# A two-layer hybrid decoder trunk on one core: one layer end for all layers, and two GpSimd subtractions moved to VectorE

## The reference, cut to what matters

```python
for l in range(2):
    sh_m, sc_m, g_m, sh_f, sc_f, g_f = split(silu(c) @ ada_w[l] + ada_b[l], 6)
    proj = (rms_norm(x, norm_mix_g[l]) * (1 + sc_m) + sh_m) @ w_in[l]
    y = concatenate([ssd(proj), mla(proj), moba(proj)])      # 512 + 256 + 256 columns, normalised by group
    x = x + g_m * (y @ w_out[l])                             # the output projection
    hf = rms_norm(x, norm_ffn_g[l]) * (1 + sc_f) + sh_f
    x = x + g_f * moe_ffn(hf, ...)                           # 16 experts, each token goes to two of them
```

## Time and profile before

| What | Value |
|---|---|
| Time, median of 3 runs (lowest, highest) | 1483.41 us (1477.52, 1484.29) |
| The profiled execution's own time | 1484.28 us |
| Its span, first to last instruction | 1482.5 us |
| PE busy | 1331.1 us (90%) |
| PEld busy | 1050.8 us (71%) |
| DVE busy | 1165.1 us (79%) |
| ACT busy | 735.0 us (50%) |
| POOL busy | 257.7 us (17%) |
| Mean granted TensorE clock | 0.949 of full speed |

### The profile page before, as it was taken

How to read it: one execution, slowest core, us unless ns; L and a number is a source line. 1 busy time by engine, 2 the same in 40 slices (tenths; PEclk the granted TensorE clock), 3 DMA queues, 4 the chain that set the end, 5 groups by cost and what they waited for, 6 DMA issues and landing times. The chain is left out here.

```text
span 1482.5 us, 17406 instructions
## 1 busy us (share of the span) xinstructions
PE 1331.1 (90%) x6467; PEld 1050.8 (71%) x6467; DVE 1165.1 (79%) x1372; ACT 735.0 (50%) x967; POOL 257.7 (17%) x300
## 2 busy tenths in 40 slices
PE   6799987869989999999949998886898999999994
PEld 3677865657878888888647777564677788888882
DVE  3669856894679999999855987398657899999985
ACT  1334343562337777777413342345413777777760
POOL 0100135461011000000120012339001110010002
PEclk9899997989999999999969999898899999999997
DMA  9676521423579999998548573133327899999955
GB/s 361 234 263 225 191 92 56 142 88 141 211 285 365 413 401 416 410 407 351 210 164 301 172 256 118 57 114 114 128 99 284 336 399 410 404 415 403 410 186 185
DMA packets 95461, 378.64 MB, mean 255 GB/s; under 512 B 5961, under 2 KB 8759, under 8 KB 85768
## 3 DMA queue, kind: packets, MB, share of 16 engines
q1 hardware_dynamic: 71816, 307.83, 54.7%
q0 software_dynamic: 15232, 55.63, 9.6%
q10 hardware_dynamic: 8320, 13.96, 2.7%
HBM read 344.58 MB, written 32.82 MB: 255 GB/s over the span
## 5 line engine op out<-in xcount | busy, mean ns | idle before, releaser
L1278 PE MATMUL ps<-mod_rounded,work_rounded 128*128 128x512 f32 x340 | 136.9, 403 | 1.1 <-DVE work_rounded L2284 1.1
L1280 PE MATMUL ps<-mod_rounded,work_rounded 128*128 128x512 f32 x340 | 134.6, 396 | 0.0
L1739 DVE SCALAR_TENSOR_TENSOR gain<-ring,csil,gain 128x512 f32<-128x512 f32 x134 | 111.6, 833 | 3.3
L1279 PE MATMUL ps<-ring_rounded,work_rounded 128*128 128x512 f32 x288 | 113.9, 396 | 0.0
L2143 DVE TENSOR_TENSOR ring_rounded<-ring,mod_rounded 128x2048 fp32r<-128x2048 f32 (+1 forms) x54 | 102.9, 1930 | 1.4
L1279 PE MATMUL ps<-work_rounded 128*128 128x512 f32 x256 | 101.0, 395 | 0.0
L2143 DVE TENSOR_TENSOR work_rounded<-work,mod_rounded 128x2048 fp32r<-128x2048 f32 (+1 forms) x48 | 91.3, 1931 | 9.9 <-ACT mod_rounded L1638 8.7
L2527 POOL DMA_INDIRECT work<-ffn_rows,slot_idx x34 | 42.0, 1236 | 302.8 <-PE ps L1264 270.1
L929 PE MATMUL ps<-ring_rounded,actT_rounded 128*128 128x512 f32 (+1 forms) x256 | 93.9, 367 | 0.0
L1638 ACT ACTIVATE mod_rounded<-ring 128x2048 fp32r<-128x2048 f32 (+1 forms) x54 | 85.9, 1625 | 0.0
L929 PE MATMUL ps<-work_rounded,mod_rounded 128*128 128x512 f32 (+1 forms) x192 | 77.1, 401 | 4.0 <-ACT work L1405 4.0
(11 more groups left out here) (371 smaller groups left out, 3647.2 us busy)
## 6 DMA issues: line engine op xcount, KB each, us to landing
ring<-in_ada_w SPq DMA_DIRECT2D x38, 1024.0 KB, 5.3
ring<-in_moe_w_gate SPq DMA_DIRECT2D x18, 2048.0 KB, 10.0
ring<-in_moe_w_up SPq DMA_DIRECT2D x18, 2048.0 KB, 10.4
ring<-in_moe_w_down SPq DMA_DIRECT2D x18, 2048.0 KB
work<-in_moe_w_up SPq DMA_DIRECT2D x16, 2048.0 KB, 10.7
work<-in_moe_w_down SPq DMA_DIRECT2D x16, 2048.0 KB, 11.6
work<-in_moe_w_gate SPq DMA_DIRECT2D x16, 2048.0 KB, 10.2
expert_rows<-work POOLq DMA_DIRECT2D x32, 512.0 KB, 7.9
```

What stands on the lines that cost most here:

```text
L1278: pe.matmul(ps[j][:, :], xl, hi, start=k == 0, stop=False)
L1279: pe.matmul(ps[j][:, :], xh, lo, start=False, stop=False)
L1280: mm = pe.matmul(ps[j][:, :], xh, hi, start=False, stop=k == KD - 1)
L1739: add(v.scalar_tensor_tensor(acc, w, csil[:, k:k + 1], acc, ALU.mult, ALU.add))
```

## The change

1. The low halves (0, 1) and (1, 0) of the output weights are made by VectorE: (0, 1) in step n = 25 of the heads, (1, 0) after the last early `y_low` and ahead of the wait for the norm. GpSimd's loop and its semaphore are gone, and PE waits for `out_w_lo` to reach 1, 2, 3, 4 in the order of the halves.
2. At the layer's end the branches on L are gone from SP, ScalarE and VectorE: layer 1 too loads "the next layer's" first block (of layer 0 again), rows and gain, splits the block and scales the gain. Nothing reads these.
3. The eight adds of slot 16 and their products stand once, after `If(nov > 1)` instead of before it. Within that branch each further tile first adds the tile before it.

```diff
-                with sp.If(L < DEPTH - 1):
-                    load_first_in(sp, (L + 1) % DEPTH)
-                    sp.dma_start(mod[:, 0:2 * D], ...).then_inc(next_b, 16)
-                    sp.wait_ge(y_ps, 2 * (NTL - 1))
-                    load_mix_gain(sp, (L + 1) % DEPTH)
-                    sp.wait_ge(next_b, 16)
+                load_first_in(sp, (L + 1) % DEPTH)
+                sp.dma_start(mod[:, 0:2 * D], ...).then_inc(next_b, 16)
+                sp.wait_ge(y_ps, 2 * (NTL - 1))
+                load_mix_gain(sp, (L + 1) % DEPTH)
+                sp.wait_ge(next_b, 16)
...
-                OUT_LOW = [(out_w_lo, 1), (out_w_lo_g, 1), (out_w_lo_g, 2), (out_w_lo, 2)]
-                            pe.wait_ge(*OUT_LOW[2 * b + k // 4])
+                            pe.wait_ge(out_w_lo, 2 * b + k // 4 + 1)
...
-                for b in range(2):
-                    pe.wait_ge(y_ev, 2 * (NTL - 1) + b + 1)
-                    for t in range(T):
-                        by_token(b, t).then_inc(cb_ps, 1)
                 with pe.If(nov > 1):
...
+                for b in range(2):
+                    pe.wait_ge(y_ev, 2 * (NTL - 1) + b + 1)
+                    for t in range(T):
+                        by_token(b, t).then_inc(cb_ps, 1)
...
-                with a.If(L < DEPTH - 1):
-                    a.wait_ge(y_ps, 2 * (NTL - 1))
-                    first_in_hi(a)
+                a.wait_ge(y_ps, 2 * (NTL - 1))
+                first_in_hi(a)
...
-                    if n == 19:
-                        out_weights_lo(0, 0)
+                    if n in (19, 25):
+                        out_weights_lo(0, (n - 19) // 6)
                     late_adds(n)
...
                     y_low(q)
+                out_weights_lo(1, 0)
                 v.wait_ge(yrs, 3)
...
-                with v.If(L < DEPTH - 1):
-                    last_out(True)
-                with v.If(L > DEPTH - 2):
-                    last_out(False)
+                e = NTL - 1
+                first_in_lo(v, 0, 2 * (len(IN_ORDER) - 1))
+                y_out(e, e % 2, halves=(0,))
+                first_in_lo(v, 1, 2 * (len(IN_ORDER) - 1))
+                y_out(e, e % 2, halves=(1,))
+                v.wait_ge(next_b, 16)
+                mix_gain(v)
                 with v.If(nov > 1):
...
+                for b in range(2):
+                    for t in range(T):
+                        v.wait_ge(cb_ps, T * b + t + 1)
+                        add_by_token(0, b, t)
...
-                for b, half in ((0, 1), (1, 0)):
-                    g.wait_ge(out_w_hi, 2 * b + half + 1)
-                    raw, lo, hi = out_part(b, half)
-                    g.tensor_tensor(lo, raw, hi.bitcast(F32), ALU.subtract).then_inc(out_w_lo_g, 1)
```

More of the change, by code:

```diff
@@ L832, in _ @@
                 sp.wait_ge(row_st[2], 16)
-                with sp.If(L < DEPTH - 1):
-                    load_first_in(sp, (L + 1) % DEPTH)
-                    sp.dma_start(mod[:, 0:2 * D], mod_rows[bass.ds(L + 1, 1), 0:2 * D].broadcast_to([P, 2 * D])
-                                 ).then_inc(next_b, 16)
-                    sp.wait_ge(y_ps, 2 * (NTL - 1))
-                    load_mix_gain(sp, (L + 1) % DEPTH)
-                    sp.wait_ge(next_b, 16)
+                load_first_in(sp, (L + 1) % DEPTH)
+                sp.dma_start(mod[:, 0:2 * D], mod_rows[bass.ds(L + 1, 1), 0:2 * D].broadcast_to([P, 2 * D])
+                             ).then_inc(next_b, 16)
+                sp.wait_ge(y_ps, 2 * (NTL - 1))
+                load_mix_gain(sp, (L + 1) % DEPTH)
+                sp.wait_ge(next_b, 16)
                 nov = sp.value_load(ctl[0:1, 0:1], min_val=0, max_val=NOV)
@@ L1330, in by_token @@
                                      start=True, stop=True)
-                for b in range(2):
-                    pe.wait_ge(y_ev, 2 * (NTL - 1) + b + 1)
-                    for t in range(T):
-                        by_token(b, t).then_inc(cb_ps, 1)
                 with pe.If(nov > 1):
+                    pe.wait_ge(y_ev, 2 * NTL)
                     with pe.Fori(0, NOV - 1) as i:
                         with pe.If(nov > i + 1):
+                            for b in range(2):
+                                for t in range(T):
+                                    by_token(b, t).then_inc(cb_ps, 1)
                             pe.wait_ge(ov_x, i + 1)
@@ L2327, in add_by_token @@
                     return v.scalar_tensor_tensor(x_, ps[2 * t + b][:, :], over_w[:, t, n:n + 1], x_, ALU.mult, ALU.add)
[L2329 to L2344, removed]
                 hidden(NTL - 1)
@@ L2359, in _ @@
                         with v.If(nov > n):
+                            for b in range(2):
+                                for t in range(T):
+                                    v.wait_ge(cb_ps, 2 * T * (n - 1) + T * b + t + 1)
+                                    ins = add_by_token(n - 1, b, t)
+                            ins.then_inc(ov_x, 1)
                             v.wait_ge(ov_si, n)
@@ L2363, in _ @@
                             slot_tokens(n)
+                            v.wait_ge(ov_x, n)
+                            v.tensor_copy(over_w[:, :, 0:1], over_w[:, :, n:n + 1])
                             v.wait_ge(ov_yp, n)
@@ L2366, in _ @@
                             v.tensor_tensor(ysb[:, 0, 512:1024], ps[7][:, :], gf[:, 512:1024], ALU.mult).then_inc(ov_ye, 1)
-                            for b in range(2):
-                                for t in range(T):
-                                    v.wait_ge(cb_ps, 2 * T * n + T * b + t + 1)
-                                    ins = add_by_token(n, b, t)
-                            ins.then_inc(ov_x, 1)
+                            v.wait_ge(cb_ps, 2 * T * (n + 1))
+                for b in range(2):
+                    for t in range(T):
+                        v.wait_ge(cb_ps, T * b + t + 1)
+                        add_by_token(0, b, t)
             @block.gpsimd
```

1 line of the change is left out of this document (removed).

## The result

| | Before | After |
|---|---|---|
| Time, median of 5 runs (lowest, highest) | 1483.41 us (1477.52, 1485.46) | 1472.33 us (1469.03, 1477.23) |
| The profiled execution's own time | 1484.28 us | 1472.33 us |
| Its span | 1482.5 us | 1470.7 us |
| DVE busy | 1165.1 us | 1162.9 us |
| POOL busy | 257.7 us | 239.1 us |

The ratio is 0.9934, with a 95% interval from 0.9912 to 0.9957: faster by 11 us, beyond the 0.5% that the forecast wanted. The forecast was 1472.7.

A forecast was written before the change was run, and what follows sets the result against it. In the heads VectorE, held up by GpSimd's subtractions, was taken to bound all engines. -15.6 + 4.6 + 0 - 1.0 + 0 + 1.3 = -10.7 us from 1484.28 gives 1473.6, as a median 1472.7; range 1465.5 to 1479.5.

The forecast's parts named there:

- GpSimd's subtractions gone, half (0, 1) in step 25: Heads, both layers: -15.6 us of VectorE waiting under GpSimd, +4.6 us for VectorE making the half itself.
- the prediction's sign: Heads: biased(28) 5.3 us earlier after the heads' start in layer 0, 5.7 in layer 1; output products 5 to 6 earlier.
- Half (1, 0) at no cost: After the last early column block: VectorE's 2.29 us fit its 2.95 us wait for GpSimd's norm, cost 0.
- The slow clock behind the hole: Heads, after PE's idle stretch: part of the low granted clock goes, -0.5 us per layer, -1.0 in sum.
- End of layer 0: Layer 0's end: GpSimd arrives last and covers what moves on VectorE and PE, 0 us, bounds -3.0 and +3.0.
- rival 2: Layer ends: the skips were dear, -3 us in layer 0 and -1 in layer 1, 1467.4 us; chance 0.12.
- End of layer 1: Layer 1's end: loads delay gathers by 4.4 us, barrier 1.8 us later less a 0.5 us skip, +1.3 us.
- rival 1: Layer ends: uncovered skip before PE's products, +1 us in layer 0, +4.4 in layer 1, total 1477; chance 0.17.
- the prediction's own signs: Layer 1's end: right if 5 to 7 us follow the last add; wrong if down-products-to-next-layer time changes over 3 us.
- The hole: Heads: stretch where GpSimd's subtractions hold up VectorE and PE idles 8.10 us in layer 0, 7.49 in layer 1.
- rival 3: Heads: the hole is not the path, so the 11 us are only moved, 1483 us; chance 0.06.
- Rival 4: Layer 1's end: slot 16's products wait for the useless 2 MB load, 11.2 us later, 1483.9 us; chance 0.04.

The follow-up runs named there:

- e1: The kernel before with only the move of the two low halves to VectorE, layer ends as before: 1472.72 us, ratio 0.9946 to the kernel before.
- e2: The kernel before with only the new layer end; GpSimd keeps its two subtractions: 1484.35 us, ratio 1.0020 to the kernel before.
- e7: The changed kernel with half (0, 1) back on GpSimd, half (1, 0) still on VectorE: 1476.46 us, ratio 0.9968 to the kernel before.
- e6: The changed kernel with half (1, 0) back on GpSimd, half (0, 1) still on VectorE: 1490.12 us, ratio 1.0039 to the kernel before.
- e0: The repetition: the changed kernel run once more, unaltered, beside the other variants: 1476.42 us, ratio 0.9959 to the kernel before.
- e5: The kernel before with the move alone, half (0, 1) in step 24, layer ends as before: 1469.08 us, ratio 0.9898 to the kernel before.
- e8: The changed kernel with two extra VectorE instructions of 1.22 us before slot 16's adds: 1478.22 us, ratio 0.9962 to the kernel before.
- e3: The changed kernel with the branches on L back, slot 16's adds still behind If(nov > 1): 1472.83 us, ratio 0.9945 to the kernel before.
- e10: The changed kernel with layer 1's 2 MB block load and split branched out again, rows and gain still loaded: 1472.91 us, ratio 0.9937.

## Why the prediction was right

**What the forecast was against what came.** 1472.7 was predicted; the first pair gave 1472.33, and the ratio of the repetition, 0.9959, puts it near 1477. Both lie in the range. "Faster" (below 1476.0) holds by the first pair; by the repetition the change gives 0.4% and falls just short of it. The mechanism of the gain was right, two terms were mis-sized (the end of layer 1 for a wrong reason), and luck hid it: of the 11.8 us between the two traces only 7.6 net lie in stretches that the change touches.

- **GpSimd's subtractions gone, half (0, 1) in step 25 (-15.6 + 4.6).** Right. `biased(28)` was to come 5.3 and 5.7 us earlier; it came 4.9 and 5.8, counted from step 24. Counted from the start of the heads, as the prediction's sign has it, it came 3.6 and 10.4 us earlier, because steps 0 to 4 ran at other clocks. The output products start 4.7 and 6.3 us earlier after step 24 (at 333.11 and 1039.68 for 336.80 and 1056.25), for the 5 to 6 of the sign. The half took 2.29 us as the earlier trace rows had it, the sums shrank to the medians of the earlier trace rows. `e1` and `e2` separate it from the rest, `e7` and `e6` repeat the blocking with one subtraction each.
- **Half (1, 0) at no cost.** Right. It lies in the wait for the norm, which comes 336.47 - 333.06 = 3.4 us after the column block instead of 2.95: GpSimd's first small norm instruction took 0.66 us instead of 0.20 (the kernel before, at 338.35) and ended just behind VectorE's half. That cost nothing: from step 31 to the last down products both traces take 399.0 us in layer 0 and 399.2 in layer 1. The Trainium skill ("SBUF — State Buffer", section "SBUF: two separate sides") says that a VectorE instruction with two SBUF inputs and a GpSimd one that reads SBUF exclude one another for a whole instruction; that fits these rows and those of `e6`. The blocked instruction of `e7`, a TENSOR_SCALAR, has one such input, as has the first long one of the earlier trace rows, so where the prediction lets the rows of the long sums agree with that rule, this holds for the other three only. The same section of the Trainium skill names a second case, a VectorE instruction in a performance mode that takes both ports, but no row here says which mode it ran in. VectorE was left 1.21 us of idle time, not 0.7, because the half ended before the norm's longer second instruction began.
- **The slow clock behind the hole (-1.0).** Too large, and for a reason: the low clock was to go with PE's long wait, and it stayed. Steps 28 to 31, the nearest stretch behind it, took +0.2 and -0.5 us, at a granted clock of 0.79 and 0.72 before and 0.77 and 0.77 after, and `e0` shows 8.73 and 9.25 us there, more than before. The clock does count in these steps, more than the prediction had it. In layers 0 and 1 of `e5` they run at the 1.2 and at the 2.4 GHz level and take 10.74 and 6.70 us; at the lower level PE is busy for 10.52 us of the 10.74, at the upper one VectorE for 6.52 of the 6.70. The first row here is the changed kernel's layer 0; the columns are the window, its length, the busy time of PE, PEld, DVE, ACT and POOL, and the clock in front of the DMA share:

```profile
318.46:326.55 8.09, 7.52 (x41) 6.28 (x41) 6.80 (x16) 5.01 (x12) 0.00 (x0) 0.77 0.00 0
```

```profile
315.29:326.03 10.74, 10.52 (x39) 8.41 (x40) 6.89 (x17) 4.63 (x11) 0.00 (x0) 0.50 0.00 0
1029.65:1036.35 6.70, 6.04 (x41) 4.88 (x41) 6.52 (x16) 5.04 (x13) 0.00 (x0) 1.00 0.00 0
```

- **End of layer 0 (0).** Right within a microsecond: -0.9, which is rival 2's direction at less than a third of its size. Across the runs taking the branches out saved some 0.8 us here (`e6` left out).
- **End of layer 1 (+1.3).** This step failed. "The barrier would then be met 1.8 us later" set GpSimd's delay of 4.4 us against the adds, as if the adds had closed the layer before and GpSimd had 2.6 us to spare. It had none. In the kernels without the loads adds that end 1.5 us later move the last block by 0.2 us at most, `e8` shows the same for the changed kernel with 2 us, and in all runs the last block follows GpSimd's last gather by 7.2 to 8.2 us. The delay itself was forecast well (gathers' end at 16.9 us after the down products, forecast 16.7) and counts in full: +4.6, less the 0.3 us that the exit after it got shorter. It is rival 1's price, by another mechanism: rival 1 named the skip in front of PE's products, which by `e3` costs nothing. Two of the prediction's own signs say so: 10.96 us lie between the last add and the last block, not 5 to 7, and the distance from the last down products changed by 4.3 us, beyond the 3 us that it had named as a sign of being wrong.

The errors add to some 3 us (+3.0 at the end of layer 1, +0.7 for the clock, -0.9 in layer 0, +0.3 in steps 24 to 28), which would have made the forecast 1476. The sign of the whole stood on steps 24 to 28, which were forecast well.

**The other rivals.** The hole was the path (rival 3 out). Slot 16's rows did not wait for the 2 MB: it landed in 8.0 us, and VectorE's first half waited 1.82 us for ScalarE's high part in layer 1 and 1.72 in layer 0. Rival 4's late landing did not occur in any trace (7.7 to 8.0 us in the kernels with the load in layer 1); its 21.2 us of the earlier trace rows was a load of `ada_w`, not of this block.

## What to carry to other kernels

When a long two-input instruction of GpSimd runs beside VectorE's SBUF sums, look for one sum per subtraction that takes as long as it: moving 4.5 us of GpSimd work to 2.3 us of VectorE work freed the larger part, and putting it where VectorE waits anyway made it nearly free (0.7 us, and nothing behind the heads). Work and loads that nobody reads are not free because an engine has room: ask what store or gather shares the queue and who waits for that. At a barrier the engine to watch is the one after whose last work the exit comes at a constant distance, which only several traces or a deliberate delay show; the idle time of the others says nothing.

## What was not expected of the hardware

**The same code at different clocks.** Steps 0 to 4 of the heads are the same in all these kernels. In 24 such stretches (12 traces, two layers) they took 17.4 us nine times, 18.8 to 19.0 three times, 20.0 to 20.1 four times, and 21.8 to 21.9 eight times. Granted clock (the column before the DMA share) inside this stretch, the changed kernel's layer 0 (21.8 us) and layer 1 (17.4 us):

```profile
205.00:216.00 11.00, 11.00 (x24) 5.02 (x23) 1.00 (x4) 3.92 (x10) 0.00 (x0) 0.64 0.00 0
917.00:925.00 8.00, 8.00 (x28) 3.93 (x27) 1.74 (x5) 4.56 (x11) 0.00 (x0) 1.00 0.00 0
```

0.64 is a mix of the 1.2 and the 2.4 GHz level, 1.00 is the 2.4 GHz level, and PE is busy all the time in both. So which level a stretch gets is not set by the code alone. Between the fastest and the slowest of these stretches lie 4.5 us in each layer, up to 9 us in an execution, which is as much as this change is worth; a sum of one trace against another has to be cut at such stretches, and a ratio of few runs can be off by some microseconds, as the first one was.

**A small instruction is blocked like a large one.** Before the change a sum over one row (1x512) took 4.87 us under GpSimd's subtraction; in the changed kernel the same lines have a median of 0.69 us. Sums over 128x512 took 4.51, 4.57 and 5.00 us, so here the size of the blocked instruction played no part.

**VectorE lengthens GpSimd's DMA issues.** A gather that began while VectorE was in a two-input instruction of 1.2 or 2.3 us took 1.2 to 2.5 us to issue instead of 0.94. In `e10` the gain's instruction (1441.61 to 1442.83) overlaps two gathers too, but one had begun before it and one began 0.18 us before its end, and they took 0.94 and 0.99 us.

**A store of 512 KB behind 3.5 MB of loads** took 6.4 us to land instead of 2.9, though the block of 2 MB had been issued about 7 us before it. Behind 1.5 MB it took 4.0 us; there the rows (1 MB) had landed before the store was issued, and only the gain's 0.5 MB were still on their way.
